# Two-layer attention with values as the stationary operand: two heads weighed side by side, probabilities kept in strips, outputs made transposed

## What is computed

```python
# differential attention, block of 128 queries
sc = einsum('bqhcd,bkhcd->bhcqk', q_blk, k) * scale - slopes * dist      # c: two softmaxes
pr = softmax(sc);  attn = pr[:, :, 0] - lam * pr[:, :, 1]
o  = einsum('bhqk,bkhd->bqhd', attn, v)                                  # 64 wide
o  = rmsnorm(o over the head's 64 columns, g_sub) * (1 - lam_init)
# window attention: keys of the block before, the own and the next
e  = exp(sc - m);  pr = e / (sum(e) + exp(sink - m))
o  = einsum('bnkgqc,bnckd->bnqkgd', pr, v)
y  = concat([y_a, y_b, y_c]) @ w_out
```

## Time and profile before

| what | value |
|---|---|
| median of 3 runs (lowest, highest) | 3331.32 us (3329.55, 3334.09) |
| the profiled execution's own time | 3329.13 us |
| its span, first to last instruction | 3327.3 us |
| PE busy | 3264.0 us, 98% |
| DVE, ACT, POOL busy | 1198.6, 1173.9, 1656.1 us (36, 35, 50%) |
| attention of layer 0, layer 1 (scores of slot 0 to the end of the partial products in the tail) | 154.94 us, 155.33 us |

### The profile page before, as it was taken

One profiled execution on the slowest core, in us unless ns is written; L12 is line 12 of the kernel. 1 busy time (PEld: TensorE's weight loads), 2 busy tenths in 40 slices (PEclk: granted clock), 3 DMA queues, 4 the chain that ended last, 5 costly groups with the idle time before them and its releaser, 6 DMA issues.

```text
span 3327.3 us, 43878 instructions
## 1 busy us (share of the span) xinstructions
PE 3264.0 (98%) x15940; PEld 2689.6 (81%) x15940; DVE 1198.6 (36%) x1891; ACT 1173.9 (35%) x1860; POOL 1656.1 (50%) x917
## 2 busy tenths in 40 slices
PE   8999999999999999999999999999999999999998
PEld 6778888787788887888888788888888887688887
DVE  4534114555441145511345332124311443331134
ACT  4743223448432234422333432222322233332222
POOL 6735444667254446644456244444544453354444
PEclk9999999999999999999999999999999999999999
DMA  4112222231122222322223122222222222122222
GB/s 152 45 45 97 99 95 96 82 111 39 43 92 100 95 95 82 124 95 95 101 82 102 51 70 92 98 95 96 100 98 95 96 94 70 64 93 96 95 97 68
DMA packets 82400, 293.87 MB, mean 88 GB/s; under 512 B 9035, under 2 KB 11467, under 8 KB 82028
## 3 DMA queue, kind: packets, MB, share of 16 engines
q1 hardware_dynamic: 80944, 286.06, 24.8%
q10 hardware_dynamic: 1340, 6.23, 0.5%
HBM read 290.15 MB, written 2.10 MB: 88 GB/s over the span
## 4 chain that ended last, share of the span: by engine, by line
PE 87%; POOL 5%; DVE 3%; issue 3%; ACT 1%; DMA 0%; SPq 0%; POOLq 0%; DVEq 0%; ACTq 0%
PE bank L2036 27%; PE bank L2038 27%; PE bank L2037 27%; POOL w_lo L566 2%; PE bank L2529 1%; POOL scr L624 1%; POOL diag L705 1%; PE bank L2490 1%; PE bank L2510 1%; PE bank L2352 0%; POOL small L618 0%; PE bank L2330 0%; DVE y L1624 0%; DVE mvl L1372 0%; POOL big L640 0%
## 5 line engine op out<-in xcount | busy, mean ns | idle before, releaser
L566 POOL TENSOR_TENSOR w_lo<-w_raw,w_hi 128x1024 fp32r<-128x1024 f32 (+1 forms) x541 | 1307.8, 2421 | 1480.7 <-ACT w_hi L800 1480.5
L2036 PE MATMUL bank<-mvh,w_hi 128*128 128x512 f32 (+1 forms) x4536 | 1741.9, 384 | 34.5 <-DVE mvl L1326 13.9
L2038 PE MATMUL bank<-mvh,w_lo 128*128 128x512 f32 (+1 forms) x4536 | 1716.6, 378 | 0.0
L2037 PE MATMUL bank<-mvl,w_hi 128*128 128x512 f32 (+1 forms) x4536 | 1716.0, 378 | 0.0
L800 ACT ACTIVATE w_hi<-w_raw 128x1024 fp32r<-128x1024 f32 x537 | 568.3, 1060 | 1739.8 <-PE bank L2038 1736.9
L2036 PEld LDWEIGHTS bank<-mvh,w_hi 128*128 128x128 f32 x4536 | 853.9, 188 | 225.2 <-issue 38.3
L2038 PEld LDWEIGHTS bank<-mvh,w_lo 128*128 128x128 f32 x4536 | 853.7, 188 | 161.1
L2037 PEld LDWEIGHTS bank<-mvl,w_hi 128*128 128x128 f32 x4536 | 854.7, 188 | 152.0 <-issue 0.2
L1435 DVE TENSOR_TENSOR scr<-bank,rstd_b 128x512 f32<-128x512 f32 x264 | 181.2, 690 | 994.9 <-PE bank L2038 994.7
L1452 DVE TENSOR_TENSOR mvl<-big,mvh 128x512 fp32r<-128x512 f32 x132 | 270.0, 2056 | 346.7 <-ACT mvh L930 346.7
L705 POOL TENSOR_TENSOR diag<-diag,scr 128x256 f32<-128x256 f32 (+1 forms) x146 | 160.2, 1098 | 25.3 <-ACT scr L818 12.7
(11 more groups left out here) (198 smaller groups left out, 1511.3 us busy)
## 6 DMA issues: line engine op xcount, KB each, us to landing
w_raw<-in_weights SPq DMA_DIRECT2D x537, 512.0 KB, 3.2
x<-in_x SPq DMA_DIRECT2D x8, 256.0 KB, 8.0
out_y<-y SPq DMA_DIRECT2D x8, 256.0 KB, 2.2
tab<-in_dist ACTq DMA_DIRECT2D x2, 640.0 KB
tab<-in_gmlp ACTq DMA_DIRECT2D x2, 640.0 KB
tab<-in_ret_dil ACTq DMA_DIRECT2D x1, 1280.0 KB
y<-in_p ACTq DMA_DIRECT2D x2, 512.0 KB, 3.4
y<-in_rotary ACTq DMA_DIRECT2D x1, 1024.0 KB
```

Of the source, the lines that this page charges most:

```text
L566: last = nc.gpsimd.tensor_tensor(w_lo[:, slot, at], w_raw[:, slot, at], w_hi[:, slot, at].bitcast(F32), ALU.subtract)
L2036: nc.tensor.matmul(bank[:, at], hi, mvh[:, k, at], start=first, stop=False, skip_group_check=again)
L2037: nc.tensor.matmul(bank[:, at], hi, mvl[:, k, at], start=False, stop=False, skip_group_check=again)
L2038: return nc.tensor.matmul(bank[:, at], lo, mvh[:, k, at], start=False, stop=last, skip_group_check=again)
```

## The change

The two attentions get another way of weighing values, and what hangs on it:

- **Probabilities in strips.** The copies out of PSUM go to strips: for differential attention `diff_probs(e)`, four tiles of `big` for each of the two heads of a tile t, that hold the transposed probabilities of all four query blocks (512 columns); for window attention `window_probs(e)`, three rows of `scr` with the three heads that share a value head (384 columns). The odd copy is now DVE's in every slot. A strip has one buffer, so a copy of the next t or block waits for the weighing (`home_free`).
- **Groups go by head tile first** (`qb, t = m % 4, m // 4`), so that a strip is full after four slots.
- **`weigh_diff(l, t)`** in slots 5, 9 and 13: the stationary operand is the 128x64 tile of values of one head, the moving one the 512-wide strip; the two heads go to the lower and the upper half of the partitions of one bank. **`weigh_window(l, qb)`** in slots 16, 19, 22 and in the tail does the same with 384 columns. Outputs arrive transposed.
- **The norm across partitions.** For the differential part DVE takes the output out (slots 5, 9, 13), ACT squares it (6, 10, 14), PE transposes the squares (`diff_turn`, 6, 10, 15), DVE sums them out of PSUM and POOL makes the root (7, 11, 15), DVE spreads the root to 512 columns, PE transposes that (`diff_spread`) and DVE multiplies (all three in 8, 12, 16). For the window part DVE adds the sums and writes their reciprocal 384 columns wide (16, 19, 22, 24), PE transposes it, ACT copies it out, and DVE multiplies (17, 20, 23, tail). The transposes of outputs (L2572, L2666) are gone; `w_out`'s rows are laid out by the new order of window heads on the host.
- **The slots are dealt out anew** (`WORK`).

```diff
-                self.qb, self.t = m // 3, m % 3
+                self.qb, self.t = (m % TB, m // TB) if self.diff else (m // 3, m % 3)
...
-        WORK = [(3, 2)] * 8 + [(2, 2)] * 8 + [(0, 0)] * 4 + [(1, 1)] * 5
+        WORK = ([(3, 3)] * 5 + [(0, 0)] + [(3, 3)] * 3 + [(0, 0)] + [(3, 3)] * 3 + [(1, 1)] * 3 + [(0, 0)] * 4
+                + [(1, 1)] * 5)
...
-        SWA_ON = {16: 0, 19: 1, 22: 2}
-        SWA_OUT = {19: 0, 21: 1, 23: 2}
+        SWA_PV = {16: 0, 19: 1, 22: 2}
+        SWA_ON = {16: 0, 19: 1, 22: 2, 24: 3}
+        SWA_SPREAD = {17: 0, 20: 1, 23: 2}
+        SWA_OUT = {19: 0, 22: 1, 24: 2}
...
+        def home_free(eng, l, p):
+            g, e = pair(p)
+            if g.diff and g.t:
+                eng.wait_ge(a_pv, 7 * l + g.t)
+            if not g.diff and g.qb:
+                eng.wait_ge(a_pv, 7 * l + 3 + g.qb)
...
# ScalarE, attention_slot, at the end of a slot
+                if n in DIFF_SQUARE:
+                    t = DIFF_SQUARE[n]
+                    act.wait_ge(o_taken, 3 * l + t + 1)
+                    nc.scalar.activation(diff_squares(t), diff_out[t], ACT.Square).then_inc(osq_ready, 1)
...
+                if n in SWA_SPREAD:
+                    window_copy(l, SWA_SPREAD[n])
...
# VectorE, attention_slot
+                nc.vector.reciprocal(window_rows.rearrange("p (t e d) -> p t e d", e=2, d=64),
+                                     sink_c[:, 0:H].rearrange("p (e t) -> p t e", e=2).unsqueeze(3).broadcast_to(
+                                         [P, 3, 2, 64])).then_inc(window_rec, 1)
...
+                if n in DIFF_SPREAD:
+                    t = DIFF_SPREAD[n]
+                    dve.wait_ge(osq_rstd, 3 * l + t + 1)
+                    nc.vector.tensor_copy(diff_squares(t).rearrange("p (g d) -> p g d", d=64),
+                                          orstd.unsqueeze(2).broadcast_to([P, 8, 64])).then_inc(orstd_wide, 1)
+                if n in SWA_SPREAD:
+                    window_normalised(l, SWA_SPREAD[n])
+                if n in DIFF_SPREAD:
+                    t = DIFF_SPREAD[n]
+                    dve.wait_ge(orstd_spread, 3 * l + t + 1)
+                    dve.wait_ge(o_taken, 3 * l + t + 1)
+                    nc.vector.tensor_tensor(diff_out[t], diff_bank(t)[:, :], diff_out[t], ALU.mult).then_inc(diff_normed, 1)
...
# TensorE, attention_slot
                 if n <= DIFF_GROUPS:
                     products(0)
-                    if n >= 2:
-                        weigh_values(even - 1)
+                    if n in DIFF_PV:
+                        weigh_diff(l, DIFF_PV[n])
...
                     products(1)
+                    if n in DIFF_SPREAD:
+                        diff_spread(l, DIFF_SPREAD[n])
                     if n:
-                        weigh_values(even)
                         transpose_probs(odd)
+                    if n in DIFF_TURN:
+                        diff_turn(l, DIFF_TURN[n])
...
+            def weigh_diff(l, t):
...
+                for kb in range(TB):
+                    for e in range(2):
+                        last = nc.tensor.matmul(banks[OUT][64 * e:64 * e + 64, :], tok(AV + t, kb, 64 * e, 64),
+                                                diff_probs(e)[:, kb, :], start=(kb == 0), stop=(kb == TB - 1))
+                last.then_inc(a_pv, 1)
```

More of the change, by code:

```diff
@@ L177, in program @@
         shift = diag[:, 1, 0:16]
-        osum, orstd, o_v, o_t = (small[:, 232 + 6 * i:238 + 6 * i] for i in range(4))
+        osum, orstd, o_v, o_t = (small[:, 320 + 8 * i:328 + 8 * i] for i in range(4))
         norm_stats = diag[:, 0, 0:96]
@@ L1193, in _ @@
                     attention_slot(l, n)
+                window_copy(l, TB - 1)
                 window_high(l, TB - 1)
@@ L2599, in attention_slot @@
                     products(p % 2)
-                    weigh_values(p - 1)
+                    if n in DIFF_SPREAD and p == even:
+                        diff_spread(l, DIFF_SPREAD[n])
+            def weigh_diff(l, t):
+                pt_ready(pe, l, 8 * t + 6)
+                pt_ready(pe, l, 8 * t + 7)
+                if t == 0:
+                    pe.wait_ge(vt_copied, 6 * l + 3)
+                else:
+                    pe.wait_ge(diff_normed, 3 * l + t)
+                for kb in range(TB):
[3 more added lines that the diff above has]
+                last.then_inc(a_pv, 1)
@@ new lines, in diff_turn, with diff_spread @@
+            def diff_turn(l, t):
+                pe.wait_ge(osq_ready, 3 * l + t + 1)
+                if t == 2:
+                    pe.wait_ge(mix_taken, 2 * l + 2)
+                for b in range(TB):
+                    last = nc.tensor.transpose(diff_bank(t)[:, b * P:(b + 1) * P],
+                                               diff_squares(t)[:, b * P:(b + 1) * P], ident[:, :])
+                last.then_inc(osq_turned, 1)
+            def diff_spread(l, t):
+                pe.wait_ge(orstd_wide, 3 * l + t + 1)
+                for b in range(TB):
+                    last = nc.tensor.transpose(diff_bank(t)[:, b * P:(b + 1) * P],
+                                               diff_squares(t)[:, b * P:(b + 1) * P], ident[:, :])
+                last.then_inc(orstd_spread, 1)
@@ new lines, in weigh_window @@
+            def weigh_window(l, qb):
+                p = DIFF_PAIRS + 6 * qb + 4
+                pt_ready(pe, l, p)
+                pt_ready(pe, l, p + 1)
+                if qb == 0:
+                    pe.wait_ge(vt_copied, 6 * l + 6)
+                    pe.wait_ge(diff_normed, 3 * l + 2)
+                    pe.wait_ge(o_taken, 3 * (l + 1))
+                else:
+                    pe.wait_ge(onorm_ready, w_block(l, qb))
+                kb0, kb1 = max(0, qb - 1), min(TB, qb + 2)
+                for i in range(kb1 - kb0):
+                    for e in range(2):
+                        last = nc.tensor.matmul(banks[OUT][64 * e:64 * e + 64, 0:3 * P], tok(CV, kb0 + i, 64 * e, 64),
+                                                window_probs(e)[:, i, 0:3 * P], start=(i == 0),
+                                                stop=(i == kb1 - kb0 - 1))
+                last.then_inc(a_pv, 1)
@@ new lines, in window_rows_of @@
+            def window_rows_of(l, qb):
+                pe.wait_ge(window_rec, w_block(l, qb) + 1)
+                if qb == 0:
+                    pe.wait_ge(diff_normed, 3 * (l + 1))
+                else:
+                    pe.wait_ge(window_copied, w_block(l, qb))
+                for t in range(3):
+                    last = nc.tensor.transpose(banks[MISC][:, t * P:(t + 1) * P],
+                                               window_rows[:, t * P:(t + 1) * P], ident[:, :])
+                last.then_inc(window_spread, 1)
@@ L2863, in weight_units @@
         out.append(tiles_of(np.concatenate([w[:, :swa0], q, w[:, swa0 + 384:]], axis=1))[list(A_TILES)])
-        out.append(tiles_of(i["w_out"][l]))
+        rows = [640 + 64 * h + d for h in order for d in range(64)]
+        out.append(tiles_of(np.concatenate([i["w_out"][l][:640], i["w_out"][l][rows]], axis=0)))
         ffn(i["w_ffn_in"][l][:, :FT * P], i["w_ffn_in"][l][:, FT * P:], i["w_ffn_out"][l])
```

213 lines of the change are left out of this document (84 added, 129 removed).

## The result

Median of 4 runs 3352.53 us (3351.82 to 3355.93), before 3331.29; the ratio is 1.0065, 95% interval 1.0048 to 1.0082. The change makes the kernel slower by 21.2 us, 0.65%. The forecast was 3337, no change close to slower, range 3313 to 3353. By the prediction's own line of 6.7 us the kernel is plainly slower, a case to which it had given 0.35.

The account below looks back on a forecast made before the run. PE, busy 98% of the span, was taken as the bound. Per layer -32.4 + 18.5 + 1.1 - 5.3 + 20.8 of waits = +2.7 us, twice +5.4, giving 3337 us, range 3313 to 3353.

Parts of the forecast that it names:

- the prediction's own line of 6.7 us: Whole kernel: a measurement tells 0.2% (6.7 us) from no change; chances faster 0.25, same 0.40, slower 0.35.
- Two of the prediction's own signs: Right: attention at 157 to 158 us a layer; wrong: a reciprocal over 1 us.
- PE's work: Per layer: weighing removed -32.4, weighing added +18.5, transposes +1.1 us.
- slots 5 and 9: No products there; odd transposes wait for ACT's copy of the even ones' bank, 0.6 each, 1.2 us.
- Slots 6 and 10: `diff_turn` waits for a square at the end of ACT's queue, 2 x 1.8 = 3.6 us.
- Slots 8 and 12: `diff_spread` waits for the root's spread copy, 1.9 and 2.4, together 4.3 us; bounds 0.2 and 5.
- Slot 9: `weigh_diff(1)` waits for the copy of pair 15, queued on DVE behind the held copy: 0.8 us.
- Window slots and tail: Slots 16 to 19, 21 and tail: PE waits on DVE and ACT queues, together 10.9 us, 5 to 14 possible.
- The held copy: Slots 8 and 12: POOL's w_lo holds DVE's spread copy of the root; 1.9 and 2.4 us lost.
- The wide reciprocal: Rival, window blocks: DVE's 384-wide reciprocal takes 2.6 us, not 0.55; 8 us more, 3345; chance 0.12.
- the ports free: Rival: ports don't collide, 4.1 us a layer come back in slots 8, 9 and 12; 3329; chance 0.13.

Follow-up runs that it names:

- run 9: The change with small reciprocal, later squares, POOL waiting, DVE's window order and low parts moved, value copy earlier, two products in slots 5 and 9; 3306.5 us.
- Run 1: The change with a 128x6 window reciprocal and a copy that spreads it, in place of the 384-wide reciprocal; 3348.6 us.
- run 5: The kernel before, with only the window's reciprocal written 384 wide and then multiplied as before; 3351.2 us against 3331.0.
- 11: run 9 with slot 8's odd pair's copy taken by DVE ahead of the gated MLP's normalisation; 3307.4 us.

## Why the prediction was right, and where it was wrong

The direction and the range held, but the size did not: 5.4 us more were forecast and 21.2 measured. That the range still held, by 0.5 us, is luck. Its upper end was set by the long reciprocal together with a part of the held waits, not by what filled the gap. Two of the prediction's own signs went against it: a reciprocal of over 1 us appeared, and the attention took 167.3 and 165.6 us a layer where 157 to 158 was to show the forecast right. The step that failed is one that the sum never had: **PE's work was priced at full clock throughout**, since the window showed 1.00, while the same text put 20.8 us of waits into it.

*PE's work.* Forecast -12.8 a layer. At full clock (run 9, layer 0) it is 135.07 where it was 149.39, -14.3. `weigh_diff` cost 3.6 a block, forecast 3.7; `weigh_window` at full clock 2.16 for twelve records, forecast 2.17. The tiles do run side by side.

*The clock.* The change's PE work was 144.29 and 141.61. Against 135.07 that is 9.2 and 6.5 us of slow work, 15.7 in all; of before, layer 1 had 1.0 of it. The Trainium skill's "TensorE: Matmul & The Clock Gate", "Part 1: The HAM clock gate (the "warmup" mystery)", says that the array's default is the low clock and that activity releases it. These runs agree in the main: in the tail and the window slots the clock fell to 1.2 GHz behind waits of 1.9 to 3 us, and it came back with dense work. But waits of 1.87 and 1.88 in slots 8 and 10 left it at 1.00.

*The waits,* term by term, layer 0, forecast then measured: slots 5 and 9, 1.2 and 1.56 (twice 0.78). Slots 6 and 10, 3.6 and 3.42. Slots 8 and 12, 4.3 and 4.14. Slot 9, 0.8 and 0.63. Window slots and tail, 10.9 and 10.8. Missed: the odd transposes of slots 3 and 4, 2.06, which wait for ACT's value copy; the weighing that used to stand there (0.83) had covered it. With the small ones, 20.8 against 23.0, in layer 1 24.0.

*The window term was right by errors that cancel.* Slot 16 was put down to w_lo; there it was the long reciprocal. Run 1 shows that both stood in line: without the one, the other takes its place at the same 2.6. Slots 17 to 19 were forecast 4.2 + 3.3 and took 3.1 + 2.2, slot 21 and the tail were forecast 1.0 and took 2.9.

*The held copy.* Forecast as held, from rows of a two-source instruction and of a pair; 2.58 and, freed, 0.43. The Trainium skill's "SBUF — State Buffer", section "Who interferes with whom", counts copies among the instructions that can take the port pair shared with GpSimd, and these two times agree with it. (With the ports free the prediction took 4.1 a layer off, for slots 8, 9 and 12; that is the two roots alone, and slot 9's 0.8 would have come on top.)

*The wide reciprocal.* A rival with 0.12. Its slope from the earlier trace rows, 6.4 ns a column, gave 2.6 and 2.55 was measured; small rows are indeed mostly fixed cost, by this slope some 154 of the 160 ns, but their difference gave the slope rightly all the same. The estimate from the Trainium skill's "VectorE: DVE Perf Modes", section "First, the fixed hardware budget", was 3.2; the measurement decides. What the rival got wrong is its price in the change: it counted 2.05 in two places, 8 us. Run 1 gets back 3.9, since in slot 16 the held copy takes the reciprocal's place. In the kernel before, run 5 measures 20.2 (22.1 between the profiled executions: 12.5 of waits, 9.8 of slow work in the two layers).

The books of the span: waits 47.0 against 41.6 forecast, +5.4; PE's work at full clock -3.0; the clock +15.7, less the 1.0 that before had. That is 17.1, and 22.6 measured less 5.4 forecast is 17.2.

What stays open: what decides whether the clock falls behind a wait of some 2 us. Behind 2.27 in slot 12 the change shows both in one execution, behind 1.8 runs 9 and 11 show both, and no experiment here tells them apart.

## What to carry to other kernels

When a change takes work from the bounding engine, the other engines' queues decide what comes back, and on TensorE every wait that is left may be paid a second time in clock: price the work behind each wait of two us at both levels and keep the sum of the low one in the range. A single mend can understate its part, because a freed wait runs into the next one and, more so here, because the clock may not come back until several waits are gone. So mend them together before judging a change: this one, 21 us slower as written, ended 23.5 us faster than the kernel before once a copy, a root and the low parts stood in the right order. Keep element-wise reciprocals small and spread them with a copy.

## What the runs showed of the hardware

- A reciprocal on DVE costs 160 ns for one column, 192 for 6 and 2553 for 384: 6.2 ns a column, where a copy of 384 takes 0.55 us.
- A one-source copy of 128x512 from a broadcast took 0.43 us alone, and 2.58 when it began 0.06 behind POOL's subtraction; the long reciprocal, begun at 181.11 with a w_lo beside it from 181.64 on, kept its 2.55.
- The granted clock fell behind waits in PE's queue with column tiles and without them (0.72 in the change's slots 16 to 19, 0.86 in run 5's window slots), and behind the same wait of 2.27 us it fell in one layer (0.82) and not in the other (1.00) of one execution. In the kernel before with the long reciprocal 6.3 us of waits a layer cost 5.2 and 4.6 us of slow work on top.
